# The gate/up stage of a hybrid decoder layer: chunk 3 in place of chunk 7 as the one split by an accumulating DMA

## Chip, cores and metric

The kernel runs on one core of one Trainium2 chip. The metric is the device time of one execution in microseconds, as the median of several runs. TensorE (PE) does the matrix products, DVE (VectorE), ACT (ScalarE) and POOL (GpSimd) work on the operands, SP (SyncE) issues most transfers.

## What is computed

One decoder layer for 256 tokens of width 2048, all in float32: an input projection, three kinds of token mixing, an output projection, and then the feed-forward part, which the change touches:

```python
h = rms_norm(x, ffn_norm)
return x + (jax.nn.silu(h @ w_gate) * (h @ w_up)) @ w_down
```

D_FF is 5632, so w_gate and w_up are 2048 x 5632 each and w_down is 5632 x 2048. A final RMS norm follows.

## The kernel before

**Three products for one.** TensorE multiplies in the format fp32r. To keep float32's accuracy each operand is split: hi = the value rounded to fp32r, lo = value - hi. A product is then three matmuls: x_hi with w_hi, x_hi with w_lo, x_lo with w_hi (`group`, L1665 to L1673). The weights come from memory as raw float32. ScalarE copies raw to hi (`prep_hi`, L739 and L743), DVE subtracts to make lo (`prep_lo`, L1239 and L1261).

**The gate/up stage.** It runs over FS = 11 iterations, i = 0 to 10, each for 512 columns of w_gate and the same of w_up. An iteration has FB = 8 chunks, p = 0 to 7. A chunk is 1 MB of weights (128 partitions x 4 blocks x 512 columns). Banks 0 to 3 of PSUM gather gate and up for the two halves of the tokens, bank[0] and bank[1] the gate, bank[2] and bank[3] the up part.

**Sums chunks.** Chunks 0, 2, 4, 5 (`SUMS`) are done with seven block products in place of eight, by Winograd's form of Strassen's scheme: 7 x 3 = 21 matmuls (`sums_chunk`). For this DVE first adds blocks of raw weights (L1251, L1254, L1256, into t_sum), ScalarE makes t_hi of them (L747), and DVE t_lo (L1266): the "tops". The three bare blocks get w_hi by L743 and w_lo by L1261. A sums chunk adds into banks 0 to 2 and 4 to 7. When the last of the four is done, banks 4 to 7 must be mixed: ScalarE copies bank 4 (L864), DVE makes the mix sums (`mix_sums`, L1354, L1356, L1359) and corrects banks 0 and 1, then 2 and 3 (`mix_banks`, L1369). TensorE waits for the first correction (`mixed`) before the first product of chunk 7, and for the second before its third.

**Plain chunks.** The others (1, 3, 6, 7) are 24 matmuls each (`plain_chunk`).

**The ring.** Raw weights have four slots, and so have w_hi and w_lo (w_lo lies over raw). `ring(n)` is the number of chunk n within the ring, `slot_user(n)` the chunk that had its slot before; SP issues a load (L397) when TensorE has used that chunk (`chunk_used`). SP does its loads strictly in the written order. AHEAD = 3 is how many chunks ScalarE and DVE prepare ahead of TensorE.

**The chunk set apart.** Chunk 7 (`BY_DMA`) of each iteration isn't in the ring. SP loads it into d_raw (L407), ScalarE makes d_hi (`apart_hi`, L844), then writes -d_hi into d_lo (`apart_negated`, L849; d_lo lies over d_raw), and GpSimd issues a DMA that reads the chunk from memory once more and adds it to d_lo (L479). What it leaves is lo, without any work of DVE. TensorE waits for `lo_added`. In the kernel before all this is done within the iteration: d_raw is loaded when the iteration before is used up, and ScalarE does its two steps beside chunks 3 to 5.

**End of an iteration.** When chunk 7 has filled a bank, ScalarE makes the gate (L870, Silu), DVE multiplies it with the up part (L1454). In the next iteration TensorE turns this tile after chunk 0 and within chunk 1 (`hidden_turn`, L1564), and ScalarE stores it (`keep_hidden`, L816).

**Down stage.** 44 chunks m of w_down go through the same ring (`down_hi`, `down_lo`). Chunk 0 is a sums chunk whose sums are made at the end of iteration 10. After the load of down chunk 3 SP waits for the end of the gate/up stage and brings back x (2 MB, x_keep, L423), which was put away to make room for d_raw, d_lo and d_hi.

## Time and profile before

| | us |
|---|---|
| median of 3 runs | 1106.45 |
| lowest, highest | 1102.81, 1107.13 |
| the profiled execution, its time | 1107.73 |
| the profiled execution, its span | 1105.2 |
| TensorE busy | 1083.0 (98%) |
| DVE busy | 909.5 (82%) |
| ScalarE busy | 652.5 (59%) |

The granted TensorE clock is 0.995 of full on the mean. The gate/up stage runs from about 387 to 866 us of the span, the down stage from there to the end. Busy shares tell little here, since TensorE is busy nearly always: the profile is read by its waits, by who releases them, and by what that engine did before. In a timeline row the bracket at the end holds the idle time before the instruction and its releaser; "PE" rows are matmuls, "SPq" rows the issue of a transfer, and "128x2048 fp32r<-128x2048 f32" is result and source.

### The profile page before, as it was taken

What the parts mean: (1) busy time and instruction counts of PE and PEld (TensorE: products, weight loads), DVE (VectorE), ACT (ScalarE), POOL (GpSimd) and SP (SyncE); (2) the same over time, 40 slices, a digit from 0 to 9 for tenths busy, and PEclk for the clock granted to TensorE, in tenths of its full rate; (3) what the DMA queues carried; (4) which work ended last, traced back from release to release, by engine and by line L of the source; (5) the groups of instructions that cost most, each with busy time, mean ns of one, the idle gap of its engine ahead of it and who ended that gap; (6) DMA issues with size and microseconds to landing.
All of it is one profiled execution on the core that took longest, in us unless ns stands there. A gap on an engine that the chain in (4) does not pass through costs nothing.

```text
span 1105.2 us, 12406 instructions
## 1 busy us (share of the span) xinstructions
PE 1083.0 (98%) x5094; PEld 898.8 (81%) x5094; DVE 909.5 (82%) x858; ACT 652.5 (59%) x639; POOL 57.4 (5%) x55
## 2 busy tenths in 40 slices
PE   9999999999999998999999999999999999999997
PEld 6888889987888877877887887887888788888886
DVE  6889666754666798898898898998998799998995
ACT  7666446656655565664664664655657455565553
POOL 0078000000000000000000000000000000000000
PEclk9999999999999999999999999999999999999999
DMA  8765644653445586766766757757667665555552
GB/s 330 278 232 201 201 120 137 199 174 118 143 162 191 191 304 196 244 193 232 239 196 222 243 198 245 224 194 243 205 228 237 233 210 205 190 195 206 208 192 113
DMA packets 50439, 228.55 MB, mean 207 GB/s; under 512 B 4304, under 2 KB 10192, under 8 KB 28752
## 3 DMA queue, kind: packets, MB, share of 16 engines
q1 hardware_dynamic: 47936, 213.84, 55.8%
q0 software_dynamic: 1584, 11.54, 5.6%
q10 hardware_dynamic: 864, 2.39, 0.6%
q8 instruction: 40, 0.66, 0.2%
q14 instruction: 15, 0.12, 0.0%
HBM read 223.56 MB, written 4.19 MB: 206 GB/s over the span
## 4 chain that ended last, share of the span: by engine, by line
PE 82%; DMA 6%; DVE 5%; issue 3%; ACT 3%; SPq 0%; DVEq 0%; ACTq 0%
PE ps L1672 61%; PE ps L1525 5%; PE ps L1527 5%; PE ps L1526 5%; DMA raw<-in_w_gu 5%; PE ps L1564 2%; ACT w_hi L739 1%; DMA d_raw<-in_w_gu 1%; DVE mix L1356 1%; DVE t_sum L1251 1%; DVE ps L1369 1%; PE ps L1612 1%; PE ps L1789 1%; PE ps L1790 1%; PE ps L1791 1%
## 5 line engine op out<-in xcount | busy, mean ns | idle before, releaser
L1672 PE MATMUL ps<-w_hi,xp_hi 128*128 128x512 f32 x396 | 156.1, 394 | 3.0 <-DVE t_lo L1266 3.0
L966 DVE TENSOR_TENSOR w_lo<-raw,w_hi 128x2048 fp32r<-128x2048 f32 (+2 forms) x42 | 87.3, 2078 | 86.6 <-ACT w_hi L490 86.6
L1672 PE MATMUL ps<-w_hi,xp_lo 128*128 128x512 f32 x396 | 154.3, 390 | 0.0
L1672 PE MATMUL ps<-w_lo,xp_hi 128*128 128x512 f32 x396 | 154.2, 389 | 0.0
L747 ACT ACTIVATE t_hi<-t_sum 128x2048 fp32r<-128x2048 f32 x44 | 84.4, 1917 | 90.9 <-DVE t_sum L1256 90.9
L830 ACT ACTIVATE w_hi<-raw 128x2048 fp32r<-128x2048 f32 (+1 forms) x44 | 79.2, 1800 | 77.6 <-DMA raw<-in_w_dn 77.6
L1672 PE MATMUL ps<-w_hi,xo_hi 128*128 128x512 f32 x292 | 113.8, 390 | 0.0
L1672 PE MATMUL ps<-w_hi,xo_lo 128*128 128x512 f32 x292 | 113.6, 389 | 0.0
L1672 PE MATMUL ps<-w_lo,xo_hi 128*128 128x512 f32 x292 | 113.6, 389 | 0.0
L1266 DVE TENSOR_TENSOR t_lo<-t_sum,t_hi 128x2048 fp32r<-128x2048 f32 x44 | 100.8, 2290 | 12.0 <-ACT t_hi L747 12.0
L490 ACT ACTIVATE w_hi<-raw 128x2048 fp32r<-128x2048 f32 (+2 forms) x42 | 73.0, 1739 | 49.5 <-DMA raw<-in_w_out 25.8
L1239 DVE TENSOR_TENSOR w_lo<-raw,w_hi 128x2048 fp32r<-128x2048 f32 x33 | 75.6, 2290 | 22.6 <-ACT w_hi L739 22.6
L1672 PEld LDWEIGHTS ps<-w_hi,xp_hi 128*128 128x128 f32 x396 | 74.5, 188 | 18.1 <-DVE t_lo L1266 3.4
L1672 PEld LDWEIGHTS ps<-w_hi,xp_lo 128*128 128x128 f32 x396 | 74.3, 188 | 15.7
L1672 PEld LDWEIGHTS ps<-w_lo,xp_hi 128*128 128x128 f32 x396 | 74.4, 188 | 14.9
L1384 DVE TENSOR_TENSOR w_lo<-raw,w_hi 128x2048 fp32r<-128x2048 f32 x32 | 73.2, 2288 | 14.4 <-ACT w_hi L830 14.3
L1261 DVE TENSOR_TENSOR w_lo<-raw,w_hi 128x1536 fp32r<-128x1536 f32 x44 | 77.3, 1756 | 2.1 <-ACT w_hi L743 1.0
L743 ACT ACTIVATE w_hi<-raw 128x1536 fp32r<-128x1536 f32 x44 | 65.4, 1487 | 22.8 <-DMA raw<-in_w_gu 22.8
L739 ACT ACTIVATE w_hi<-raw 128x2048 fp32r<-128x2048 f32 x33 | 63.0, 1909 | 26.0 <-DMA raw<-in_w_gu 26.0
L1672 PE MATMUL ps<-t_hi,xp_hi 128*128 128x512 f32 x176 | 69.1, 392 | 0.4 <-DVE xp_lo L1208 0.4
L1672 PE MATMUL ps<-t_hi,xp_lo 128*128 128x512 f32 x176 | 69.2, 393 | 0.0
L1672 PE MATMUL ps<-t_lo,xp_hi 128*128 128x512 f32 x176 | 69.2, 393 | 0.0
(294 smaller groups left out, 2471.0 us busy)
## 6 DMA issues: line engine op xcount, KB each, us to landing
raw<-in_w_gu SPq DMA_DIRECT2D x77, 1024.0 KB, 4.9
raw<-in_w_dn SPq DMA_DIRECT2D x44, 1024.0 KB, 4.9
raw<-in_w_i SPq DMA_DIRECT2D x21, 1024.0 KB, 4.9
raw<-in_w_out SPq DMA_DIRECT2D x16, 1024.0 KB, 5.2
raw<-in_w_in SPq DMA_DIRECT2D x12, 1024.0 KB, 5.1
d_raw<-in_w_gu SPq DMA_DIRECT2D x11, 1024.0 KB, 4.9
d_lo<-in_w_gu POOLq DMA_DIRECT2D x11, 1024.0 KB, 9.1
raw<-in_w_in SPq DMA_DIRECT2D x8, 576.0 KB, 3.8
```

Source lines behind the costliest of these rows:

```text
L490: nc.scalar.activation(w_hi[n % 4][:, 0:k, 0:c], raw[n % 4][:, 0:k, 0:c], ACT.Copy).then_inc(hi_ready, 1)
L739: nc.scalar.activation(w_hi[slot][:], raw[slot][:], ACT.Copy).then_inc(hi_ready, 1)
L743: nc.scalar.activation(w_hi[slot][:, 1:4, :], raw[slot][:, 1:4, :], ACT.Copy).then_inc(hi_ready, 1)
L747: nc.scalar.activation(t_hi[s % 2][:], t_sum[s % 2][:], ACT.Copy).then_inc(tops_hi, 1)
L830: nc.scalar.activation(w_hi[slot][:, blocks, :], raw[slot][:, blocks, :], ACT.Copy).then_inc(hi_ready, 1)
L966: nc.vector.tensor_tensor(w_lo[n % 4][:, 0:k, 0:c], raw[n % 4][:, 0:k, 0:c], w_hi[n % 4][:, 0:k, 0:c].bitcast(F32), ALU.subtract).then_inc ...
L1239: nc.vector.tensor_tensor(w_lo[slot][:], raw[slot][:], w_hi[slot][:].bitcast(F32), ALU.subtract).then_inc(lo_ready, 1)
L1261: nc.vector.tensor_tensor(w_lo[slot][:, 1:4, :], raw[slot][:, 1:4, :], w_hi[slot][:, 1:4, :].bitcast(F32), ALU.subtract)
L1266: nc.vector.tensor_tensor(t_lo[s][:], t_sum[s][:], t_hi[s][:].bitcast(F32), ALU.subtract).then_inc(lo_ready, 1)
L1384: nc.vector.tensor_tensor(w_lo[slot][:], raw[slot][:], w_hi[slot][:].bitcast(F32), ALU.subtract).then_inc(lo_ready, 1)
L1525: nc.tensor.matmul(out, hi, w_h, start=start, stop=False)
L1672: mm = nc.tensor.matmul(out, x, wt, start=start and j + m == 0, stop=stop and 3 * j + m == n - 1, skip_group_check=resumed)
```

## The change

Chunk 3 in place of chunk 7 is set apart, in iterations 1 to 10. In iteration 0 all eight chunks go through the ring, so that there are ten accumulating DMAs in place of eleven. The chunk of iteration i + 1 is prepared in iteration i: SP loads d_raw behind the load of chunk 7, when chunk 3 has been used; ScalarE does apart_hi before its copy of bank 4 and the negation behind it; GpSimd's DMA follows. The ring has chunks 0 to 2 and 4 to 7 in each iteration from 1 on. The loops of ScalarE and DVE over p are written out in another order: DVE does all low parts of an iteration, then the mix sums, then the next iteration's sums of chunk 0, the first correction, the low part of its bare blocks, the second correction, the tops, the gates, and only then chunk 1. Before, the next iteration's sums stood ahead of the mix sums, its bare low part ahead of both corrections, and chunk 1 ahead of the gates.

Core of the diff (the first hunks: constants, ring, SP, GpSimd; then ScalarE's ffn, DVE's prep_lo and ffn, TensorE's):

```diff
-BY_DMA = 7
+BY_DMA = 3
...
-    return n - sum(FF0 + BY_DMA + FB * i < n for i in range(FS))
+    return n - sum(FF0 + BY_DMA + FB * i < n for i in range(1, FS))
...
-    return next(m for m in range(n) if ring(m) == r and not (FF0 <= m < DN0 and (m - FF0) % FB == BY_DMA))
+    return next(m for m in range(n) if ring(m) == r and not (FF0 + FB <= m < DN0 and (m - FF0) % FB == BY_DMA))
...
-                if i == 0:
+                if i == 1:
                     sp.wait_ge(x_kept, 16)
                     sp.wait_ge(unit_filled, len(ORDER))
                     sp.wait_ge(nx2.squared, 8)
                 else:
-                    sp.wait_ge(chunk_used, FF0 + FB * i)
+                    sp.wait_ge(chunk_used, FF0 + FB * (i - 1) + BY_DMA + 1)
                 sp.dma_start(d_raw[:].rearrange("p a b -> p (a b)").unsqueeze(1),
                              w_gu[:, FB * i + BY_DMA:FB * i + BY_DMA + 1, :]).then_inc(d_in, 16)
 
             for i in range(FS):
                 for p in range(FB):
-                    if p != BY_DMA:
+                    if i == 0 or p != BY_DMA:
                         load_ring(FF0 + FB * i + p, w_gu[:, FB * i + p:FB * i + p + 1, :])
                     if i == 0 and p == 3:
                         sp.wait_ge(acc_free, ACC_O + 8)
                         sp.dma_start(t["x_keep"], xin[:].rearrange("p a b -> p (a b)")).then_inc(x_kept, 16)
-                    if p == (5 if i == 0 else 3):
-                        load_apart(i)
+                    if p == FB - 1 and i + 1 < FS:
+                        load_apart(i + 1)
...
-            for i in range(FS):
-                pool.wait_ge(negated, i + 1)
+            for i in range(1, FS):
+                pool.wait_ge(negated, i)
...
-                act.wait_ge(d_in, 16 * (i + 1))
+                act.wait_ge(d_in, 16 * i)
...
-                act.wait_ge(d_hi_made, i + 1)
+                act.wait_ge(d_hi_made, i)
...
-                        nc.scalar.activation(mix[:, 0, :], bank[4], ACT.Copy).then_inc(mix_first, 1)
...
-                    q = p + AHEAD
-                    if q == BY_DMA:
-                        if last:
-                            down_hi(0, "b")
-                        else:
-                            prep_hi(i, FB, "b")
...
-                        prep_hi(i, q, "b")
-                        if p == (2 if first else 1):
-                            apart_negated(i)
-                        prep_hi(i, q, "t")
...
-                    if p == (1 if first else 0):
-                        apart_hi(i)
+                if first:
+                    for j, u in enumerate(UNITS[FF0]):
+                        act.wait_ge(unit_filled, INDEX[u] + 1)
+                        split_pair_hi(u, late_bank[j])
+                    prep_hi(i, 2, "t")
+                    prep_hi(i, 3)
+                    root(nx2, 1, D)
+                else:
+                    keep_hidden(i, (0,))
+                    prep_hi(i, 2, "t")
+                    keep_hidden(i, (1,))
+                prep_hi(i, 4)
+                if first:
+                    prep_hi(i, 5)
+                    prep_hi(i, 6)
+                else:
+                    prep_hi(i, 5, "b")
+                    prep_hi(i, 6)
+                    prep_hi(i, 5, "t")
+                prep_hi(i, 7)
+                if not first and not last:
+                    apart_hi(i + 1)
+                act.wait_ge(mix_done, i * 2 + 1)
+                if not first:
+                    act.wait_ge(mixed, i * 2)
+                nc.scalar.activation(mix[:, 0, :], bank[4], ACT.Copy).then_inc(mix_first, 1)
+                if not first and not last:
+                    apart_negated(i + 1)
+                if last:
+                    down_hi(0)
+                else:
+                    prep_hi(i, FB)
+                if first:
+                    apart_hi(i + 1)
+                    apart_negated(i + 1)
+                    act.wait_ge(nx2.ready, 1)
+                for b in range(TOK):
+                    act.wait_ge(ffn_done, i * 3 + (b + 1))
+                    nc.scalar.activation(gate[:, b, :], bank[b], ACT.Silu,
+                                         scale=nx2.r[:, b:b + 1]).then_inc(gate_set, 1)
+                if last:
+                    down_hi(1)
+                    down_hi(2)
+                else:
+                    prep_hi(i, FB + 1)
+                    prep_hi(i, FB + 2, "b")
 
...
+                    if q == SUMS[2]:
+                        dve.wait_ge(chunk_used, i * FB + (FF0 + SUMS[0] + 1))
...
-                    if p == SUMS[-1]:
-                        ahead = (lambda parts: down_lo(0, parts)) if last else (lambda parts: prep_lo(i, FB, parts))
-                        ahead("s")
-                        mix_sums(i)
-                        ahead("w")
-                        mix_banks(i, 0, None)
-                        mix_banks(i, 1, i * FB + (FF0 + 7))
-                        ahead("l")
-                    if p == FB - 1:
-                        for b in range(TOK):
-                            dve.wait_ge(gate_set, i * 2 + (b + 1))
-                            if b == 0:
-                                dve.wait_ge(ffn_done, i * 3 + 3)
-                            else:
-                                dve.wait_ge(chunk_used, i * FB + (FF0 + FB))
-                            nc.vector.scalar_tensor_tensor(out=gate[:, b, :], in0=bank[2 + b],
-                                                           scalar=nx2.r[:, b:b + 1], in1=gate[:, b, :],
-                                                           op0=ALU.mult, op1=ALU.mult).then_inc(hid_made, 1)
-                    if p + AHEAD > FB and last:
-                        down_lo(p + AHEAD - FB)
-                    elif p + AHEAD not in (BY_DMA, FB):
-                        prep_lo(i, p + AHEAD)
...
+                else:
+                    prep_lo(i, 2)
+                for p in range(4, FB):
+                    prep_lo(i, p)
+                mix_sums(i)
+                ahead = (lambda parts: down_lo(0, parts)) if last else (lambda parts: prep_lo(i, FB, parts))
+                ahead("s")
+                mix_banks(i, 0, None)
+                ahead("w")
+                mix_banks(i, 1, i * FB + (FF0 + 7))
+                ahead("l")
+                for b in range(TOK):
+                    dve.wait_ge(gate_set, i * 2 + (b + 1))
+                    if b == 0:
+                        dve.wait_ge(ffn_done, i * 3 + 3)
+                    else:
+                        dve.wait_ge(chunk_used, i * FB + (FF0 + FB))
+                    nc.vector.scalar_tensor_tensor(out=gate[:, b, :], in0=bank[2 + b],
+                                                   scalar=nx2.r[:, b:b + 1], in1=gate[:, b, :],
+                                                   op0=ALU.mult, op1=ALU.mult).then_inc(hid_made, 1)
+                if last:
+                    down_lo(1)
+                    down_lo(2)
+                else:
+                    prep_lo(i, FB + 1)
...
-                w_h, w_l = (d_hi, d_lo) if p == BY_DMA else (m[ring(FF0 + FB * i + p) % 4] for m in (w_hi, w_lo))
+                w_h, w_l = (d_hi, d_lo) if p == BY_DMA and not first else (m[ring(FF0 + FB * i + p) % 4] for m in (w_hi, w_lo))
-                    if p == BY_DMA:
-                        pe_.wait_ge(lo_added, 16 * (i + 1))
+                    if p == BY_DMA and not first:
+                        pe_.wait_ge(lo_added, 16 * i)
```

DVE, before, from the plain low part of chunk 6 of one iteration to its gates; L1239 is a plain low part, L1251 to L1256 are sums, L1354 to L1359 mix sums, L1369 corrections, L1454 gates:

```order
L1239 TENSOR_TENSOR w_lo_54<-raw_50,w_hi_58 128x2048
L1251 TENSOR_TENSOR t_sum_61<-raw_51 128x1024
L1254 TENSOR_TENSOR t_sum_61<-t_sum_61,raw_51 128x512
L1256 TENSOR_TENSOR t_sum_61<-t_sum_61,raw_51 128x512
L1354 TENSOR_TENSOR mix<-mix,ps 128x512
L1356 TENSOR_TENSOR mix<-ps,mix 128x1024
L1359 TENSOR_TENSOR mix<-ps,mix 128x512
L1261 TENSOR_TENSOR w_lo_55<-raw_51,w_hi_59 128x1536
L1369 TENSOR_TENSOR ps<-ps,mix 128x1024 x2
L1266 TENSOR_TENSOR t_lo_63<-t_sum_61,t_hi_65 128x2048
L1239 TENSOR_TENSOR w_lo_56<-raw_52,w_hi_60 128x2048
L1454 SCALAR_TENSOR_TENSOR gate<-ps,stats,gate 128x512 x2
```

DVE, after, from the plain low part of chunk 6 on (L1356 to L1361 are now the mix sums, L1253 to L1258 sums, L1263 the bare low part, L1371 a correction):

```order
L1239 TENSOR_TENSOR w_lo_54<-raw_50,w_hi_58 128x2048
L1239 TENSOR_TENSOR w_lo_55<-raw_51,w_hi_59 128x2048
L1356 TENSOR_TENSOR mix<-mix,ps 128x512
L1358 TENSOR_TENSOR mix<-ps,mix 128x1024
L1361 TENSOR_TENSOR mix<-ps,mix 128x512
L1253 TENSOR_TENSOR t_sum_61<-raw_52 128x1024
L1256 TENSOR_TENSOR t_sum_61<-t_sum_61,raw_52 128x512
L1258 TENSOR_TENSOR t_sum_61<-t_sum_61,raw_52 128x512
L1371 TENSOR_TENSOR ps<-ps,mix 128x1024
L1263 TENSOR_TENSOR w_lo_56<-raw_52,w_hi_60 128x1536
L1371 TENSOR_TENSOR ps<-ps,mix 128x1024
L1268 TENSOR_TENSOR t_lo_63<-t_sum_61,t_hi_65 128x2048
```

Behind the plain low parts the mix sums now come first, and the first correction stands directly behind the next sums; chunk 7's low part is a second L1239 ahead of them.

ScalarE, before, from its second keep_hidden of an iteration on; L844 and L849 are the two steps for the chunk set apart, L864 the copy of bank 4:

```order
L816 ACTIVATE hid<-ps 128x512
L844 ACTIVATE d_hi<-d_raw 128x2048
L743 ACTIVATE w_hi_58<-raw_50 128x1536
L849 ACTIVATE d_lo<-d_hi 128x2048
L747 ACTIVATE t_hi_65<-t_sum_61 128x2048
L743 ACTIVATE w_hi_59<-raw_51 128x1536
L747 ACTIVATE t_hi_66<-t_sum_62 128x2048
L739 ACTIVATE w_hi_60<-raw_52 128x2048
L743 ACTIVATE w_hi_57<-raw_49 128x1536
L864 ACTIVATE mix<-ps 128x512
L747 ACTIVATE t_hi_65<-t_sum_61 128x2048
L739 ACTIVATE w_hi_58<-raw_50 128x2048
```

ScalarE, after, from the tops of chunk 4 on (L877 is the copy of bank 4, L890 the gates):

```order
L747 ACTIVATE t_hi_65<-t_sum_61 128x2048
L743 ACTIVATE w_hi_59<-raw_51 128x1536
L739 ACTIVATE w_hi_60<-raw_52 128x2048
L747 ACTIVATE t_hi_66<-t_sum_62 128x2048
L739 ACTIVATE w_hi_57<-raw_49 128x2048
L844 ACTIVATE d_hi<-d_raw 128x2048
L877 ACTIVATE mix<-ps 128x512
L849 ACTIVATE d_lo<-d_hi 128x2048
L743 ACTIVATE w_hi_58<-raw_50 128x1536
L747 ACTIVATE t_hi_65<-t_sum_61 128x2048
L890 ACTIVATE gate<-ps,stats 128x512 x2
L739 ACTIVATE w_hi_59<-raw_51 128x2048
```

The two steps for the chunk set apart moved from beside chunks 3 to 5 to both sides of the copy of bank 4, behind the high part of chunk 7 and ahead of that of the next chunk 0.

## Rows read from the trace of the kernel before

**Rows 1.** Table of waits, TensorE: total us, times, longest.

```profile
PE ps L1672 <- DVE ps L1369: 8.3, 6, 1.9
```

**Rows 2.** Timeline, TensorE: start us, length us, ..., [idle before <- releaser]; iterations 0, 5, 6, 10.

```profile
417.92 0.50 PE L1672 MATMUL ps<-w_hi,xp_hi 128*128 128x512 f32 x1 [3.01 <-DVE t_lo L1266]
...
419.80 0.63 PE L1672 MATMUL ps<-t_hi,xp_hi 128*128 128x512 f32 x1
420.23 0.63 PE L1672 MATMUL ps<-t_lo,xp_hi 128*128 128x512 f32 x1
...
642.59 0.39 PE L1672 MATMUL ps<-w_lo,xp_hi 128*128 128x512 f32 x1
642.82 0.39 PE L1672 MATMUL ps<-w_hi,xp_lo 128*128 128x512 f32 x1
643.23 0.47 PE L1672 MATMUL ps<-d_hi,xp_hi 128*128 128x512 f32 x1
...
686.95 0.47 PE L1672 MATMUL ps<-d_hi,xp_hi 128*128 128x512 f32 x1 [1.71 <-DVE ps L1369]
...
858.83 0.47 PE L1672 MATMUL ps<-d_hi,xp_hi 128*128 128x512 f32 x1 [1.89 <-DVE ps L1369]
```

**Rows 3.** Timeline, DVE, before chunk 7 of iteration 6.

```profile
676.53 2.29 DVE L1239 TENSOR_TENSOR w_lo<-raw,w_hi 128x2048 fp32r<-128x2048 f32 x1 [3.05 <-ACT w_hi L739]
678.74 1.22 DVE L1251 TENSOR_TENSOR t_sum<-raw 128x1024 f32<-128x1024 f32 x1
...
681.33 0.68 DVE L1354 TENSOR_TENSOR mix<-mix,ps 128x512 f32<-128x512 f32 x1
...
683.91 1.75 DVE L1261 TENSOR_TENSOR w_lo<-raw,w_hi 128x1536 fp32r<-128x1536 f32 x1
685.58 2.36 DVE L1369 TENSOR_TENSOR ps<-ps,mix 128x1024 f32<-128x1024 f32 x2
```

**Rows 4.** Timeline, GpSimd, SyncE and ScalarE: loads around the accumulating DMA.

```profile
662.87 0.86 POOL L479 DMA_DIRECT2D d_lo<-in_w_gu  x1 [41.54 <-ACT d_lo L849]
...
664.87 0.33 SPq L397 DMA_DIRECT2D raw<-in_w_gu  x1
...
670.31 0.33 SPq L397 DMA_DIRECT2D raw<-in_w_gu  x1
...
674.58 1.92 ACT L739 ACTIVATE w_hi<-raw 128x2048 fp32r<-128x2048 f32 x1 [3.43 <-DMA raw<-in_w_gu]
677.70 1.49 ACT L743 ACTIVATE w_hi<-raw 128x1536 fp32r<-128x1536 f32 x1 [1.20 <-DMA raw<-in_w_gu]
```

**Rows 5.** The page, DMA issues: KB each, median us to landing.

```profile
d_raw<-in_w_gu SPq DMA_DIRECT2D x11, 1024.0 KB, 4.9
```

**Rows 6.** Timeline, DVE: low part of the tops.

```profile
664.31 2.29 DVE L1266 TENSOR_TENSOR t_lo<-t_sum,t_hi 128x2048 fp32r<-128x2048 f32 x1 [0.59 <-ACT t_hi L747]
```

**Rows 7.** Timeline, ScalarE and DVE, iteration 0.

```profile
408.64 1.93 ACT L844 ACTIVATE d_hi<-d_raw 128x2048 fp32r<-128x2048 f32 x1 [2.52 <-DMA d_raw<-in_w_gu]
...
431.47 1.28 ACT L870 ACT_TABLE_LOAD   x1 [4.46 <-PE ps L1672]
...
408.36 1.22 DVE L1251 TENSOR_TENSOR t_sum<-raw 128x1024 f32<-128x1024 f32 x1
...
415.58 2.29 DVE L1266 TENSOR_TENSOR t_lo<-t_sum,t_hi 128x2048 fp32r<-128x2048 f32 x1 [1.78 <-ACT t_hi L747]
```

**Rows 8.** Down chunk 4: stretch (last column GB/s), then ScalarE, DVE, TensorE timelines.

```profile
866.00:878.00 12.00, 12.00 (x58) 9.97 (x57) 5.96 (x6) 5.46 (x7) 0.00 (x0) 1.00 0.87 311
...
878.13 1.49 ACT L830 ACTIVATE w_hi<-raw 128x1536 fp32r<-128x1536 f32 x1 [1.99 <-DMA raw<-in_w_dn]
...
878.47 1.22 DVE L1400 TENSOR_TENSOR t_sum<-raw 128x1024 f32<-128x1024 f32 x1
...
886.52 0.68 DVE L1429 TENSOR_TENSOR xo_lo<-sf,xo_hi 128x512 fp32r<-128x512 f32 x1
...
888.02 0.39 PE L1672 MATMUL ps<-w_hi,xo_hi 128*128 128x512 f32 x1
```

54 lines of the change are left out of this document (10 added, 44 removed).

## Prediction

> **What bounds the kernel now.** I read the table of waits first, since TensorE is busy for nearly the whole span: only what it still waits for can be gained. DVE's bank correction (L1369) holds it 8.3 us in six waits, five in iterations 1 to 9 of the gate/up stage and one in iteration 10 [rows 1]. Then TensorE's own timeline [rows 2]. A matmul lasts 0.39 us, but the next one starts after 0.23 (642.59, 642.82), so an idle time of x costs x + 0.16. The first matmul of chunk 7 starts 0.41 after the last of chunk 6 in iteration 5 (643.23), 0.18 lost; in iteration 6 (686.95) the idle time is 1.71, about 1.9 lost. Iterations 1 to 10 go on like that: six waits (8.3 + 6 x 0.16 = 9.2) and four small ones of 0.18 to 0.29 (1.0 together), in all 10.2, of which the last (858.83, 1.89 idle) has 2.05. Iteration 0 has another, 3.01 idle at 417.92, for the tops of chunk 5. Behind this one and behind 858.83 the matmuls go at 0.43 us each for a while (419.80, 420.23), which is the lower level of the clock: nine matmuls each time, 9 x 0.2 = 1.8 us. Behind the idle time of 1.71 none do.
>
> Why is the correction late? DVE's rows in iteration 6 [rows 3]: it stands 3.05 us before the low part of chunk 6, then does the next iteration's sums (678.74), the mix sums (681.33), the next low part (683.91), and only then the correction (685.58). So the 3.05, and 2.6 + 1.7 of work for the next iteration, stand ahead of what TensorE wants. The 3.05 is a transfer's [rows 4]: chunk 6 was issued at 664.87, two microseconds behind the accumulating DMA (662.87), and landed at 674.58, 9.7 later; the median is 4.9 [rows 5].
>
> **The yardstick.** A sums chunk is 21 matmuls x 0.227 = 4.76 us, a plain one 24 x 0.227 = 5.44; with 1.0 for the two turns an iteration is 4 x 4.76 + 4 x 5.44 + 1.0 = 41.8. Chunks 0 to 7 begin at T = 0, 5.2, 11.2, 16.0, 21.4, 26.2, 30.9, 36.4. DVE's steps: a plain low part 2.2 (676.53 to 678.74), sums 2.6 to 2.7, mix sums 2.6, bare low part 1.7, a correction 1.15 (two in 2.36) [rows 3]; before the tops a wait for ScalarE of 0.2 to 0.6, and their low part 2.2 [rows 6]. A sums chunk is thus about 7.0, a gate product 0.7. Per iteration 3 x 2.2 + 4 x 7.0 + 2.6 + 2.3 + 1.4 = 40.9 of 41.8: it fits, narrowly.
>
> **Iterations 1 to 9 with the change.** No work is added in them. The second gate product needs all of the chunk 7 before, so DVE starts at T = 0.1. It ends the gate at 0.8, chunk 1 at 3.0, chunk 2 at 10.2 (7.2, because keep_hidden stands before its tops on ScalarE); TensorE wants chunk 2 at 11.2. Chunk 4 ends at 17.2 (wanted 21.4), 5 at 24.2 (26.2), 6 at 26.4, 7 at 28.6. The mix sums want ScalarE's copy, which now stands behind apart_hi: d_raw is issued at 21.7, lands 4.9 later at 26.6 [rows 5], apart_hi takes until 28.5, the copy until 29.1. Mix sums to 31.7, next sums to 34.3, first correction to 35.5, wanted at 36.4; low part and second correction to 38.3, wanted at 39.1; tops of the next chunk 0 to 40.5, in time for the gates. The three narrow margins are 1.0, 0.9 and 0.8. For what is left of waits I take 0.1 per iteration, between nothing and the 0.18 of 643.23. Saved: 10.2 - 2.05 = 8.2, less 0.9, **7.3**. Bounds: 8.2, and nothing if the loads of the next paragraph are late.
>
> The moved DMA could eat this. It goes out behind the negation, at 31.4, beside the load of the next chunk 1 (31.2) and ahead of those of chunk 2 (36.6) and 4 (42.0). ScalarE wants chunk 1 at 40.7, and the margins bear it up to 41.5. The nearest rows are 4.9 and the 9.7 of old chunk 6 [rows 4, 5]: it lands between 36.1 and 40.9. I take it near 40.9, since the two transfers run together, and that is still in time. Chunk 2 is wanted at 44.8, 8.2 after its issue; the second load behind the DMA took 7.4 in the old order (670.31 to 677.70) [rows 4].
>
> A rule speaks against this. The Trainium skill (DMA: Bandwidth & Descriptors, Queues, rings and completion order) says that each DMA engine takes turns, packet by packet, between the queues that have work. A load issued together with the accumulating DMA would then share with it to the end, and be as late as the DMA itself. That is rival A, priced below from rows.
>
> **Iteration 0.** Before, ScalarE waited 2.52 us for d_raw (408.64) and did apart_hi and the negation ahead of the tops of chunk 5, which DVE began at 415.58, after 1.78 of waiting; TensorE wanted them at 417.92 - 3.17 = 414.75 [rows 2, 7]. Both steps and their transfers leave this place, and DVE goes on from the sums of chunk 5 (408.36) directly: 2.7 + 1.7 + 0.3 + 2.2, done at 415.3, wait 0.6. Then chunks 6 and 7 (2 x 2.2), mix sums, next sums and correction: 415.3 + 4.4 + 2.6 + 2.6 + 1.15 = 426.0, wanted at 415.35 + 4.76 + 5.44 = 425.5, wait 0.4, and 0.1 at the second one. Here the low part of chunk 7 is the added work (its other half was the DMA's), and it is on the path. ScalarE has the next sums at 424.7; tops, apart_hi and negation (1.8 each), the table load and the gates (1.3 each) [rows 7] end at 432.7, the high part of chunk 1 at 434.5, DVE's low part at 436.8 (wait 0.1), chunk 2 at 443.6, wanted at 442.8 (0.8). Together 2.0 to 2.1 instead of 3.2 + 1.8: saved **2.9**; bounds 5.0 (no wait) and 0.
>
> **Iteration 10.** The next sums are those of the down stage: three operations more (1.0), and 0.6 for the activations' low part before the second correction. Corrections at 36.5 (0.2 late) and 39.9 (0.7 late). It was 2.05 and 1.8 of slow clock: saved 3.85 - 0.9 = **2.95**, or 1.1 if the slow clock remains.
>
> **Down stage: a cost.** With chunk 7 in the ring, SP issues the down stage's chunk 3 when chunk 7 is used, no longer when chunk 6 is, and the return of x_keep, 2 MB, stands right behind it, then down chunk 4. Before, the return went out alone at the end of chunk 7 and down chunk 4 landed at 878.13 [rows 8]. From 866 to 878 the engines moved 311 GB/s on the mean, so one MB in front is up to 1.05/0.311 = 3.4 us; I take 3.0. Down chunk 4 was ready at 887.2 (886.52 + 0.68) for a first matmul at 888.02, 0.8 of margin, and its sums began 0.35 behind the landing (878.47). So 3.0 - 0.35 - 0.8 = **1.8** lost. Bounds 0 (other order in the queue) and 2.3.
>
> **Sum.** 7.3 + 2.9 + 2.95 - 1.8 = 11.35. The profiled execution took 1107.73 us (span 1105.2), so 1096.4 for it; it stands 1.28 over the median of the three runs, 1106.45, which becomes **1095.1**. All waits gone and no new one: 8.2 + 5.0 + 3.85 = 17.0, at 1089.4. A change within 0.5% (5.5 us: 1100.9 to 1112.0) is about what a measurement of this kernel can't tell from none.
>
> The slow stretches are 3.6 of the waits I let go, on the reading that long waits bring them: 1.71 of idle time brought none, 1.89 did [rows 2]. The Trainium skill (TensorE: Matmul & The Clock Gate, What's actually happening) says that the gate looks in windows that run freely, so one execution can fall into it where another doesn't; by that the 3.6 could stay, at 1098.7, and the two rows can't exclude it.
>
> **Rivals.**
> A, chunk 1 is late by the accumulating DMA. The nearest row for "as late as the DMA" is 662.87 to 674.58, 11.7 us with one load inside; a start together is shorter by part of it. Taken to land at 42.1 (10.9 after issue), it is 0.6 over the 41.5 that the margins bear, in each of nine iterations in place of 0.1: 9 x 0.5 = 4.5, at 1099.6. For it: 9.7 is already near 10.3. Against: old chunk 6 started two microseconds worse placed.
> B, DVE stays the bound. 40.9 of 41.8 leaves 0.9; if ScalarE's tops come 0.25 later in each sums chunk it is gone, and the period stays near the 42.9 that it has on the mean. Only iterations 0 and 10 gain and the down stage loses: 2.9 + 2.95 - 1.8 = 4.05, at 1102.4, no change.
> C, slower. The accumulating DMA holds the load of chunk 2 as well. Chunk 2 bears 8.2 + 1.0 = 9.2 us from issue to landing; beyond, all goes into TensorE's wait, nine times. 11.35/9 = 1.3 more is parity, a load of 10.5. At 11.7, the longest stretch from the DMA's issue to a landing behind it [rows 4], it is 9 x 2.5 = 22.5, at 1117.6. Against: the 7.4 of such a load.
> D, the change doesn't do what it says, since ScalarE's copy for the mix sums now hangs on d_raw. The correction bears 0.9; if d_raw lands two microseconds late, as old chunk 6 did by more, 9 x 1.1 = 10 are lost, at 1105. Against: at 21.7 the loads ahead have landed.
>
> **How the numbers follow.** Forecast (1090 to 1098) 0.52; A 0.22; B 0.12; D 0.06; C 0.08. The range leaves out C, D, a little of B and of the low end: 1090.5 to 1103. Faster by over 0.5%: the forecast, most of A and a little of B, 0.70; slower 0.08; no change 0.22.
>
> **What would show it.** Right: no idle time at chunk 7 in iterations 1 to 9, and a period of 41.8 to 41.9; a wait of 1 to 2 us at down chunk 4, its load landing some 15 us behind the end of chunk 7. Wrong: waits at chunk 1 or 2, with DVE waiting for ScalarE and ScalarE for a transfer (A, C); ScalarE idle before apart_hi and TensorE at chunk 7 (D); matmuls at 0.43 us behind no long wait (the free-running gate). What decides above all is how long the loads beside the accumulating DMA take.

## The result, and the profile after

| | before | after |
|---|---|---|
| median, us (5 runs each) | 1106.45 | 1095.2 |
| lowest, highest | 1102.81, 1107.72 | 1095.0, 1097.15 |
| time over time of before, 95% interval | | 0.9905 (0.9887 to 0.9923) |
| the profiled execution: time, span | 1107.73, 1105.2 | 1095.72, 1093.4 |
| granted clock, mean | 0.995 | 0.999 |

The forecast was 1095.1, within 1090.5 to 1103. The kernel is 1.0% faster, within the class "faster by over 0.5%". The same kernel run a second time, beside other kernels, gave 1095.93 (1095.3 to 1097.19).

The page of after: engines (busy, share, instructions), and the DMA issues with their size and time to landing.

```profile
PE 1078.3 (99%) x5094; PEld 896.6 (82%) x5094; DVE 911.8 (83%) x859; ACT 652.9 (60%) x638; POOL 55.7 (5%) x54
...
raw<-in_w_gu SPq DMA_DIRECT2D x78, 1024.0 KB, 5.0
...
d_raw<-in_w_gu SPq DMA_DIRECT2D x10, 1024.0 KB, 4.8
d_lo<-in_w_gu POOLq DMA_DIRECT2D x10, 1024.0 KB, 11.7
```

The table of TensorE's waits in after (sum, times, longest), to lay beside [rows 1]:

```profile
PE ps L1676 <- DVE xo_lo L1431: 2.1, 1, 2.1
...
PE ps L1676 <- DVE ps L1371: 0.7, 3, 0.3
PE ps L1676 <- DVE t_lo L1268: 0.7, 2, 0.5
...
PE ps L1676 <- DVE w_lo L1239: 0.2, 1, 0.2
PE ps L1676 <- ACT hid L816: 0.2, 1, 0.2
```

The 8.3 us of the bank correction are 0.7 in three waits, the 3.0 of the tops are 0.7 in two, and a new line of 2.1 stands on top, the one forecast at the down stage's chunk 4. Where these lie, in TensorE's own timeline of after; from 400 to 905 us they are all:

```profile
415.51 0.50 PE L1676 MATMUL ps<-w_hi,xp_hi 128*128 128x512 f32 x1 [0.47 <-DVE t_lo L1268]
...
426.32 0.47 PE L1676 MATMUL ps<-w_hi,xp_hi 128*128 128x512 f32 x1 [0.27 <-DVE ps L1371]
...
437.50 0.50 PE L1676 MATMUL ps<-w_hi,xp_hi 128*128 128x512 f32 x1 [0.24 <-DVE w_lo L1239]
...
442.52 0.50 PE L1676 MATMUL ps<-w_hi,xp_hi 128*128 128x512 f32 x1 [0.18 <-ACT hid L816]
...
444.37 0.51 PE L1676 MATMUL ps<-w_hi,xp_hi 128*128 128x512 f32 x1 [0.19 <-DVE t_lo L1268]
...
845.65 0.47 PE L1676 MATMUL ps<-w_hi,xp_hi 128*128 128x512 f32 x1 [0.17 <-DVE ps L1371]
...
848.96 0.50 PE L1676 MATMUL ps<-w_hi,xp_hi 128*128 128x512 f32 x1 [0.30 <-DVE ps L1371]
...
876.15 0.47 PE L1676 MATMUL ps<-w_hi,xo_hi 128*128 128x512 f32 x1 [2.07 <-DVE xo_lo L1431]
```

Between 444.37 and 845.65 there is none: iterations 2 to 9 run without a gap, one every 41.74 us. By the start-to-start times these eight waits cost 5.2 us, where before lost 16.6 in that stretch with its slow matmuls. Taken whole, from the first product of chunk 0 in iteration 0 (394.93 before, 395.06 after) to that of down chunk 4 (888.02, 876.15), before needs 493.1 us and after 481.1. So the 12.0 between the two profiled executions (1107.73 - 1095.72) all lie here, 11.4 of them in the listed waits and the slow matmuls. From 400 us on no matmul of after goes at 0.43 us.

Now DVE in iteration 6, the counterpart of [rows 3]; the iteration's first matmul is at 642.06:

```profile
665.91 4.49 DVE L1239 TENSOR_TENSOR w_lo<-raw,w_hi 128x2048 fp32r<-128x2048 f32 x2
671.15 0.69 DVE L1356 TENSOR_TENSOR mix<-mix,ps 128x512 f32<-128x512 f32 x1 [0.75 <-PE ps L1676]
...
673.74 1.22 DVE L1253 TENSOR_TENSOR t_sum<-raw 128x1024 f32<-128x1024 f32 x1
...
676.33 1.23 DVE L1371 TENSOR_TENSOR ps<-ps,mix 128x1024 f32<-128x1024 f32 x1
677.46 1.75 DVE L1263 TENSOR_TENSOR w_lo<-raw,w_hi 128x1536 fp32r<-128x1536 f32 x1
679.13 1.23 DVE L1371 TENSOR_TENSOR ps<-ps,mix 128x1024 f32<-128x1024 f32 x1
680.26 2.28 DVE L1268 TENSOR_TENSOR t_lo<-t_sum,t_hi 128x2048 fp32r<-128x2048 f32 x1
682.71 0.75 DVE L1462 SCALAR_TENSOR_TENSOR gate<-ps,stats,gate 128x512 f32<-128x512 f32 x1 [0.17 <-PE ps L1676]
684.07 0.75 DVE L1462 SCALAR_TENSOR_TENSOR gate<-ps,stats,gate 128x512 f32<-128x512 f32 x1 [0.61 <-PE ps L1676]
684.74 2.28 DVE L1239 TENSOR_TENSOR w_lo<-raw,w_hi 128x2048 fp32r<-128x2048 f32 x1
```

The 3.05 us in front of the low part of chunk 6 are gone. What DVE waits for is now TensorE: 0.75 before the mix sums, 0.17 and 0.61 before the gates. An engine that waits for the one that bounds the kernel is off the path, so this small idle time should be the margin that the new order has; two runs below test it.

ScalarE at the end of iteration 5 and the beginning of 6, where the moved transfer would show (GpSimd issued it at 631.25):

```profile
640.13 1.91 ACT L739 ACTIVATE w_hi<-raw 128x2048 fp32r<-128x2048 f32 x1
645.30 1.49 ACT L743 ACTIVATE w_hi<-raw 128x1536 fp32r<-128x1536 f32 x1 [3.27 <-DMA raw<-in_w_gu]
```

The first is the next chunk 1, which follows the gates without a wait. Its load was issued at 631.37, 0.12 us behind the accumulating DMA. Its row in SyncE's timeline, and the landing of the two from the DMA issues between 631.3 and 631.5:

```profile
631.37 0.33 SPq L397 DMA_DIRECT2D raw<-in_w_gu  x1
...
d_lo<-in_w_gu POOLq DMA_DIRECT2D x1, 1024.0 KB, 12.5
raw<-in_w_gu SPq DMA_DIRECT2D x1, 1024.0 KB, 5.8
```

The load is there at 637.2, 3 us before ScalarE comes to it, while the DMA beside it takes 12.5. The second is chunk 2, issued at 636.81: ScalarE stands 3.27 for its transfer, which lands 8.5 after its issue, and DVE's sums begin at the same 645.30, right behind the low part of chunk 1 (643.00 + 2.28). It lands just as DVE asks for it.

### The profile page after: what moved, and what is told of

It reads as the page before. It is cut to its first block, busy times and chain, and to the rows that moved or that the text cites. A ratio compares the mean times of both kernels' runs of the same rounds, so it can differ in the third digit from the quotient of the medians.

```text
span 1093.4 us, 12415 instructions
## 1 busy us (share of the span) xinstructions
PE 1078.3 (99%) x5094; PEld 896.6 (82%) x5094; DVE 911.8 (83%) x859; ACT 652.9 (60%) x638; POOL 55.7 (5%) x54
## 4 chain that ended last, share of the span: by engine, by line
PE 88%; DVE 6%; ACT 2%; DMA 2%; issue 1%; SPq 0%; DVEq 0%; ACTq 0%
PE ps L1676 67%; PE ps L1529 5%; PE ps L1531 5%; PE ps L1530 5%; PE ps L1568 2%; DMA raw<-in_w_dn 1%; DVE w_lo L1239 1%; DVE t_lo L1268 1%; ACT t_hi L747 1%; PE ps L1616 1%; DVE t_sum L1253 1%; PE ps L1793 1%; PE ps L1795 1%; PE ps L1794 1%; PE ps L1615 0%
## 5 line engine op out<-in xcount | busy, mean ns | idle before, releaser
L1676 PE MATMUL ps<-w_hi,xp_hi 128*128 128x512 f32 x404 | 159.8, 395 | 1.8 <-DVE ps L1371 0.7
L1676 PE MATMUL ps<-w_hi,xp_lo 128*128 128x512 f32 x404 | 157.5, 390 | 0.0
L1676 PE MATMUL ps<-w_lo,xp_hi 128*128 128x512 f32 x404 | 157.4, 390 | 0.0
L1239 DVE TENSOR_TENSOR w_lo<-raw,w_hi 128x2048 fp32r<-128x2048 f32 x34 | 76.7, 2284 | 1.8 <-ACT w_hi L739 1.8
L1263 DVE TENSOR_TENSOR w_lo<-raw,w_hi 128x1536 fp32r<-128x1536 f32 x44 | 77.3, 1756 | 1.1
L1676 PEld LDWEIGHTS ps<-w_hi,xo_hi 128*128 128x128 f32 x292 | 54.8, 188 | 13.8 <-DVE t_lo L1428 2.5
## 6 DMA issues: line engine op xcount, KB each, us to landing
d_lo<-in_w_gu POOLq DMA_DIRECT2D x10, 1024.0 KB, 11.7
```

The costliest lines, as they stand in the source:

```text
L1239: nc.vector.tensor_tensor(w_lo[slot][:], raw[slot][:], w_hi[slot][:].bitcast(F32), ALU.subtract).then_inc(lo_ready, 1)
L1263: nc.vector.tensor_tensor(w_lo[slot][:, 1:4, :], raw[slot][:, 1:4, :], w_hi[slot][:, 1:4, :].bitcast(F32), ALU.subtract)
L1676: mm = nc.tensor.matmul(out, x, wt, start=start and j + m == 0, stop=stop and 3 * j + m == n - 1, skip_group_check=resumed)
```

## The experiments

The question was which part of the change brings the gain of iterations 1 to 9: DVE's order, in which the correction no longer stands behind work for the next iteration, or the place of the accumulating DMA, which had run beside chunk 6's load. The prediction's sum takes the change as one schedule and doesn't tell them apart. The diffs are against the kernel named; the kernel before was run beside each group again (medians 1104.84 to 1105.9), and each ratio is to its own group's.

**DVE's order alone**, on before:

```diff
-                        ahead("s")
                         mix_sums(i)
-                        ahead("w")
+                        ahead("s")
                         mix_banks(i, 0, None)
+                        ahead("w")
                         mix_banks(i, 1, i * FB + (FF0 + 7))
```

> The kernel before with one thing of the change alone: DVE does the mix sums ahead of the next iteration's sums, and the first bank correction ahead of the next bare low part (chunk 7 stays the one set apart, within its iteration). Theory 1 (what stands ahead of the correction on DVE is half of the trouble): the correction comes 1.67 us earlier, the length of the bare low part. The six waits at chunk 7 (lost 0.96, 1.13, 1.38, 1.87, 1.83, 2.05) shrink to 0 to 0.4 each and the slow stretch behind the last one goes; the waits and slow stretch of iteration 0 (3.2 + 1.8) stay. 7 + 2 + 1.8 = about 10 us saved: 1096 to 1098, nearly the whole gain of the change. Theory 2 (the move of the transfer is what gains, DVE's order is secondary, since DVE's backlog only moves to the next wait): new waits at chunk 0 to 2 or at the second correction take most of it back, time 1102 to 1106.

Measured: 1116.91 us (1116.21 to 1118.34), 1.01 of before (1.0078 to 1.0121). A miss by 20 us, in sign too. Its waits of TensorE, DVE in iteration 6, and ScalarE there:

```profile
PE ps L1564 <- ACT hid L816: 10.4, 10, 1.1
PE ps L1672 <- DVE ps L1369: 7.1, 10, 1.9
```

```profile
682.03 2.29 DVE L1239 TENSOR_TENSOR w_lo<-raw,w_hi 128x2048 fp32r<-128x2048 f32 x1 [3.24 <-ACT w_hi L739]
684.75 0.69 DVE L1354 TENSOR_TENSOR mix<-mix,ps 128x512 f32<-128x512 f32 x1 [0.43 <-ACT mix L864]
```

```profile
658.11 1.92 ACT L747 ACTIVATE t_hi<-t_sum 128x2048 fp32r<-128x2048 f32 x1 [5.87 <-DVE t_sum L1256]
659.93 0.58 ACT L816 ACTIVATE hid<-ps 128x512 f32<-128x512 f32 x1
...
680.08 1.92 ACT L739 ACTIVATE w_hi<-raw 128x2048 fp32r<-128x2048 f32 x1 [3.62 <-DMA raw<-in_w_gu]
682.75 1.49 ACT L743 ACTIVATE w_hi<-raw 128x1536 fp32r<-128x1536 f32 x1 [0.75 <-DMA raw<-in_w_gu]
684.14 0.58 ACT L864 ACTIVATE mix<-ps 128x512 f32<-128x512 f32 x1
```

The transfer still holds DVE 3.24 at chunk 6, so the work that was moved from before the correction is done behind it, and the next iteration starts late. There ScalarE keeps the hidden layer (L816) only behind tops for which it waits 5.87 on DVE, and the turn of TensorE waits for that, ten times 1.0. And ScalarE's copy of bank 4 (L864) stands behind the next chunk's high part. Of the two theories the second had the mechanism, DVE's backlog moving to the next wait, but neither had the size. The order is worth nothing while the transfer is late: it hands the debt on.

**The move alone**, after with before's order of DVE:

```diff
-                mix_sums(i)
                 ahead = (lambda parts: down_lo(0, parts)) if last else (lambda parts: prep_lo(i, FB, parts))
                 ahead("s")
-                mix_banks(i, 0, None)
+                mix_sums(i)
                 ahead("w")
+                mix_banks(i, 0, None)
                 mix_banks(i, 1, i * FB + (FF0 + 7))
```

> The changed kernel with the old order on DVE at the end of an iteration: next sums, mix sums, next bare low part, then both corrections. Theory 1: the next chunk 0 is now loaded when chunk 4 is used (T = 26.4) and lands at 31.4, 2.8 us after DVE is through with chunk 7; with its sums ahead of the mix sums the correction ends at 31.4 + 2.7 + 2.6 + 1.7 + 1.15 = 39.5 against 36.4 wanted, so TensorE waits some 3 us at chunk 7 of every iteration: 10 x 3 = 30 us, time about 1125, and up to 15 more if each such wait brings a slow stretch of 1.8 us. Theory 2 (the transfer's place is what counts): the period stays within 0.5 us of 41.75 and the time within 5 us of the changed kernel's, 1095 to 1100.

Measured: 1148.08 us (1138.11 to 1158.6), 1.035 of before (1.0296 to 1.0398). The granted clock was 0.991 in the profiled execution, the one of 1138.11, and 0.983 to 0.967 in the three others; the expectation's 1125 to 1140 holds for the first alone. The wait, its first case with what follows, and DVE's sums for the next chunk 0 before the fourth:

```profile
PE ps L1676 <- DVE ps L1371: 34.3, 11, 4.4
```

```profile
429.09 0.47 PE L1676 MATMUL ps<-w_hi,xp_hi 128*128 128x512 f32 x1 [2.83 <-DVE ps L1371]
...
430.15 0.63 PE L1676 MATMUL ps<-w_lo,xp_hi 128*128 128x512 f32 x1
430.57 0.63 PE L1676 MATMUL ps<-w_hi,xp_lo 128*128 128x512 f32 x1
...
475.57 0.47 PE L1676 MATMUL ps<-w_hi,xp_hi 128*128 128x512 f32 x1 [2.87 <-DVE ps L1371]
...
557.48 1.23 DVE L1253 TENSOR_TENSOR t_sum<-raw 128x1024 f32<-128x1024 f32 x1 [3.05 <-DMA raw<-in_w_gu]
```

Ten waits of 2.8 to 3.2 and one of 4.4, as expected: with chunk 7 in the ring the load of the next chunk 0 goes out later (here at 552.46) and lands 3.05 us after DVE is through with chunk 7, and the old order has the sums of this chunk ahead of the mix sums, so the correction stands behind that transfer. So the new order is needed by the move, and pays nothing without it. The waits sum to 34.3; with slow matmuls the time is more than that. Matmuls at 0.43 us follow five of the eleven waits (2.83, 3.07, 3.16, 3.02, 4.40) and not the six others (2.87 to 3.11), as the first and the second here.

**The DMA taken away**, in before and in after: it moves 64 of the 2048 columns, and the low part of its chunk is left out for the rest.

```diff
-                pool.dma_start(d_lo[:].rearrange("p a b -> p (a b)"), w_gu[:, FB * i + BY_DMA, :],
+                pool.dma_start(d_lo[:].rearrange("p a b -> p (a b)")[:, 0:64], w_gu[:, FB * i + BY_DMA, 0:64],
```

> The kernel before with the accumulating DMA cut to 64 of 2048 columns (the low part of chunk 7 is left out for the rest: that part of the computation is missing, all instructions and waits stay). Theory: it is this DMA that holds the load of chunk 6 for 9.7 us in place of 4.9; without it chunk 6 lands at 5, DVE's idle 3.05 us ahead of its low part goes, and with it all waits at chunk 7: 10.2 + 1.8 saved less 0.2 to 0.5 in iteration 10, time 1094 to 1096. The wait of iteration 0 stays, since ScalarE waits there for d_raw, not for the sum. Rival: the load of chunk 6 is slow for another reason (memory, its place in the queue) or DVE's own work is the bound: then time stays at 1104 to 1107 and the 3.05 us remain.

> The changed kernel with the accumulating DMA cut in the same way (low part of chunk 3 left out). Theory: in the new place it costs nothing: ScalarE's wait of 3.27 us before chunk 2 shrinks, but TensorE waits for nothing there already, so the time stays at 1095 within 1 us. Rival: part of the period still hangs on it (waits hidden in the pace), then 1 us or more is gained.

Measured: before without it 1094.75 (1093.98 to 1098.39), 0.9902 of before; after without it 1097.56 (1095.41 to 1098.05), 0.9917 (0.9897 to 0.9936), beside 0.9905 with it. That is no faster than after; its median lies 2.4 over after's, with a granted clock of 0.997 in the three slower of its four runs, while the profiled one (1095.41) has the gaps of after to 0.03 us and the same period of 41.74. In before's place the DMA costs 11 us, in after's nothing that these runs show. Before without it, the rows that answer to [rows 3]:

```profile
667.47 2.29 DVE L1239 TENSOR_TENSOR w_lo<-raw,w_hi 128x2048 fp32r<-128x2048 f32 x1
...
679.31 1.23 DVE L1369 TENSOR_TENSOR ps<-ps,mix 128x1024 f32<-128x1024 f32 x1 [1.49 <-PE ps L1672]
```

No 3.05 in front of chunk 6, whose load takes 4.8 to 5.7 us in iterations 1 to 10 in place of 8.0 to 9.7, and in the old order the second correction waits for TensorE, though the mix sums stand behind the next sums as ever. In iterations 1 to 9 TensorE waits for no correction any more. So the whole cause of those waits is the transfer beside chunk 6's load. (Of the 3.01 at chunk 5 of iteration 0, 1.8 stay.)

**Order and ScalarE, without the move**: the first experiment, with its ScalarE faults mended (copy of bank 4 ahead of the next chunk 0's high part, the kept hidden layer ahead of the tops).

```diff
+                        prep_hi(i, 2, "t")
...
-                            prep_hi(i, FB, "b")
...
-                            prep_hi(i, FB, "t")
+                            prep_hi(i, FB)
...
+                    elif q == FB + 2:
+                        prep_hi(i, q, "b")
```

> As e1 (the kernel before with the mix sums and the first correction earlier on DVE), and ScalarE's queue put in the changed kernel's order at the two places where e1 waited: the copy of bank 4 ahead of the next chunk 0's high part, and the storing of the turned tile (keep_hidden) ahead of chunk 2's tops. Chunk 7 is still the one set apart, within its iteration. Theory (in e1 TensorE waited 10 times 1.25 us at the second turn, for keep_hidden that stood behind tops for which DVE was late): these 10 waits go, 12.5 us, but the load of chunk 6 still lands 10 to 11 us after its issue, DVE stays late, and 0.5 to 1 us at chunk 7 remain in each iteration: about 1104, no better than before. Rival (the two places on ScalarE were all that e1 lacked, and the move of the chunk isn't needed): 1095 to 1098.

Measured: 1106.26 (1101.87 to 1108.46, 10 runs), 0.9999 of before (0.9984 to 1.0013). The rival's 1095 to 1098 is excluded. The load of chunk 6 still takes 9.2 to 10.7 us in iterations 1 to 10, DVE waits 2.90 for it in iteration 6, and TensorE 4.4 in six corrections:

```profile
675.16 2.29 DVE L1239 TENSOR_TENSOR w_lo<-raw,w_hi 128x2048 fp32r<-128x2048 f32 x1 [2.90 <-ACT w_hi L739]
```

```profile
PE ps L1672 <- DVE ps L1369: 4.4, 6, 1.6
```

**How much room is there beside the moved DMA?** It is made twice in a row:

```diff
+                pool.wait_ge(lo_added, 32 * i - 16)
+                pool.dma_start(d_lo[:].rearrange("p a b -> p (a b)"), w_gu[:, FB * i + BY_DMA, :],
+                               accum_op=ALU.add).then_inc(lo_added, 16)
```

> After, with the accumulating DMA of each iteration made twice, the second behind the end of the first (the low part of bank 4's weight is then added twice, so the result is another one). It stretches the time in which a second transfer runs beside the loads of the next iteration's chunks 1, 2 and 4, from 11.7 us to over 20. If the DMA's fit depends on what it shares the engines with (rival A of the prediction, with chunk 2's load as its victim: DVE takes it the moment it lands, at 645.3): that load lands about 2 us later, chunk 2 waits 1 to 2 us in each of nine iterations, and the run takes 1105 to 1114. If the loads have room left at this place: 1096 to 1098, and no wait at chunk 2 above 0.3.

Measured: 1098.76 (1098.28 to 1099.63), 0.9939 of before (0.9917 to 0.9962), 3.6 us over after and 0.8 over the expected range. The two land 12.5 us behind their issues on the median, one after the other. All that it costs is one wait, in iteration 1, for the DMA itself:

```profile
451.86 0.50 PE L1679 MATMUL ps<-d_hi,xp_hi 128*128 128x512 f32 x1 [2.01 <-DMA d_lo<-in_w_gu]
```

and the slow matmuls behind it (1.6 us): iteration 1 takes 47.16 us there, 43.20 in after. Chunk 2 of iteration 6 is read 14.40 us behind the first DMA's issue (635.47 to 649.87) instead of 14.05 (631.25 to 645.30), and TensorE waits nowhere in iterations 2 to 9. But this doesn't test rivals A and C. The second DMA goes out 11.2 to 13.2 us behind the first; chunk 1's load had landed by then, and chunk 2's met it for a microsecond or two at most. What runs beside the second are the loads of chunks 4, 5 and 6: they take up to 10.7 us in place of 5 to 7, and TensorE waits for none of them. The room that the run shows is theirs.

**How much room does DVE have?** One operation more in an iteration, then two longer ones. The first:

```diff
+                    if not first:
+                        nc.vector.tensor_tensor(xf[:, 4:8, :], xf[:, 0:4, :], xf[:, 0:4, :], ALU.max)
                     prep_lo(i, FB + 1)
```

The second, in which the first operation is made over all eight blocks, and another stands ahead of chunk 5:

```diff
                 for p in range(4, FB):
+                    if p == 5 and 1 < i < FS - 1:
+                        nc.vector.tensor_tensor(xf[:, 0:8, :], xf[:, 0:8, :], xf[:, 0:8, :], ALU.max)
```

> After with one more DVE operation of 0.7 us (128x512 maximum, on a tile that is free) per iteration, ahead of chunk 1's low part, in iterations 1 to 9. From 605 to 647 DVE idles 0.83 ahead of the mix sums and 0.17 + 0.61 ahead of the gates, 1.61 in a period. If that idle time is real room: the operation is swallowed before the mix sums, 1095 to 1096.5. If the gate/up stage is still bound by DVE (rival B) the period grows by 0.7: 9 x 0.7 = 6.3, 1102.

> The same with two operations of 1.23 us (128x1024 maximum) per iteration, one ahead of chunk 1's low part (iterations 1 to 9) and one ahead of chunk 5's (2 to 9), 2.46 in place of 0.7. That is over the 1.61 of idle time by 0.85: about 8 x 0.85 = 7 more, 1101 to 1105, with the waits of TensorE at the corrections or at the next chunk 0. If there is more room than the idle time shows: under 1099. If DVE bounds already: 17 x 1.23 = 21, at 1116.

Measured: 1095.46 (1094.89 to 1096.58) and 1102.29 (1101.12 to 1103.3). The first is swallowed, the period still 41.74. The second has a period of 42.51, 0.77 longer, for 0.85 expected; in eight iterations that is 6.2 of the 6.8 by which it stands over the operation of 0.7 us. A period (columns: length, busy time and count of PE, PEld, DVE, ACT, POOL, then granted clock, DMA share, GB/s); first after, then with two operations:

```profile
605.44:647.18 41.74, 41.74 (x192) 34.57 (x190) 39.08 (x30) 25.49 (x18) 0.86 (x1) 1.00 0.73 228
```

```profile
529.40:571.90 42.50, 42.32 (x189) 34.35 (x189) 41.15 (x33) 25.50 (x18) 0.88 (x1) 1.00 0.71 222
```

And a row of TensorE's timeline with two:

```profile
554.80 0.47 PE L1680 MATMUL ps<-w_hi,xp_hi 128*128 128x512 f32 x1 [0.18 <-DVE ps L1371]
```

It is a wait for a correction, 0.18 to 0.22 idle and 0.33 to 0.38 lost in each iteration: the waits come back at the place where they were. The rest of the 0.77 is in losses of about 0.1 each. So the 1.61 us of idle time that DVE's rows show are its margin, right to about 0.1 (2.46 - 0.77 = 1.69).

**The return of x_keep**: after, with it in four pieces behind the down stage's chunks 6, 8, 10 and 12, and final_norm's 1 MB issued beside chunk 12 in place of chunk 0 (not in the lines below).

```diff
-                if m == 3:
-                    sp.wait_ge(chunk_used, DN0)
-                    sp.dma_start(xin[:].rearrange("p a b -> p (a b)"), t["x_keep"]).then_inc(x_back, 16)
+                if m in (6, 8, 10, 12):
+                    c = (m - 6) * 512
+                    sp.dma_start(xin[:].rearrange("p a b -> p (a b)")[:, c:c + 1024],
+                                 t["x_keep"][:, c:c + 1024]).then_inc(x_back, 16)
```

> The changed kernel with x brought back later and in four pieces of 512 KB (behind the loads of down chunks 6, 8, 10, 12) and final_norm's 1 MB issued beside down chunk 12 in place of 0. Theory: the load of down chunk 4 then takes some 5 us in place of 10, the wait of 2.07 us at down chunk 4 goes and none comes in its place: 2.2 us less than the changed kernel, 1093. Rival (the pieces hold other loads and the wait only moves): 1095.

Measured: 1094.27 (1094.18 to 1094.69), 0.9899 of before (0.9886 to 0.9913), span 1091.9 against 1093.4. That is 0.9 under after, or 1.7 under after as run beside it (1095.93); the 1093 was missed by 1.3. In the profiles the down stage's matmuls take 232.3 us from first to last in place of 234.3. The load of down chunk 4 takes 5.1 us, the wait at this chunk is gone, and no new one is listed behind it. Two transfers were moved, so the run doesn't tell apart the share of the return and that of final_norm's load.

**The ends of the stage too**: that kernel, and in iteration 0 ScalarE's apart_hi and negation around the copy and DVE's first correction ahead of the next sums; in iteration 10 the down stage's activation sums and low part behind the corrections. Then the ScalarE part alone.

```diff
+                if first:
+                    apart_hi(i + 1)
...
-                    apart_hi(i + 1)
-                    apart_negated(i + 1)
...
+                if first:
+                    mix_banks(i, 0, None)
+                    ahead("s")
+                    mix_banks(i, 1, i * FB + (FF0 + 7))
+                    ahead("w")
```

> As e6, and the order at both ends of the gate/up stage: in iteration 0 ScalarE does its two steps for the chunk set apart behind the copy of bank 4 (in its idle time before the next chunk 0's load lands), and DVE both corrections ahead of what they stood behind; in iteration 10 DVE does the activations' three sums behind the corrections. Theory: waits of 0.43, 0.23, 0.34, 0.36 (iterations 0 and 1) and 0.33, 0.46 (iteration 10) go, 2.1 us with the 2.2 of e6: 1091. Rival: in iteration 0 the accumulating DMA now runs beside the loads of chunks 1 and 2 and brings the waits back, 1092 to 1093.

> After with the return of x_keep in four pieces behind down chunks 6, 8, 10 and 12, and in iteration 0 ScalarE makes bank 4's high part and negation right around the copy, ahead of the gates and their table load (DVE as it was). The first alone gave 1094.27. Of the two waits of 0.62 and 0.43 at the end of iteration 0, the 0.43 goes if ScalarE's order is its cause, the 0.62 stays (that one is DVE's own backlog), and no wait appears at the next chunk 0: 1093.5 to 1094. If DVE's order was what brought the new 0.90 in the experiment on both, this run has none of it; if ScalarE's was, the 0.75 idle behind t_lo comes again and the time is 1094.3 or more.

Measured: 1092.47 (1092.39 to 1093.33) and, with ScalarE's part alone, 1092.61 (1091.74 to 1093.38), 0.988 of before (0.9857 to 0.9904). The first was expected at 1091 and lost part of its gain to two new waits:

```profile
431.93 0.50 PE L1687 MATMUL ps<-w_hi,xp_hi 128*128 128x512 f32 x1 [0.75 <-DVE t_lo L1269]
...
850.50 0.47 PE L1687 MATMUL ps<-w_hi,xo_hi 128*128 128x512 f32 x1 [0.87 <-DVE t_lo L1431]
```

The second has neither, so DVE's order brought them, and not the accumulating DMA as its rival had it: what was put behind the corrections was wanted right after. The second's own expectation, 1093.5 to 1094, was missed by 0.9 to the good: the 0.43 at chunk 7 of iteration 0 stays (0.46), while the three small waits of iteration 1 (437.50, 442.52, 444.37) go, which it hadn't counted on; this iteration takes 41.73 in place of 43.20 us. They came from ScalarE, whose tops, apart_hi, negation, table load and gates stood in a row ahead of chunk 1, as the prediction has it for the first of them. This is the fastest of the kernels run, 1.2% under before; the two are not told apart.

## Why the prediction was right

The forecast of 1095.1 stands beside 1095.2. That it is met to 0.1 is luck. To about 1 us it was worked out, but for what is said below of the moved DMA. The terms, by the starts of the first turn of an iteration (before: 440.07 in iteration 1, 825.24 in iteration 10, 870.76 in the down stage; after: 436.67, 813.78, 856.66) and of the two products named in the section on the result:

| saved, us | forecast | measured |
|---|---|---|
| iterations 1 to 9 | 7.3 | 9.5 |
| iteration 0, with what it leaves in iteration 1 | 2.9 | 2.1 |
| iteration 10 | 2.95 | 2.6 |
| down stage | -1.8 | -2.2 |
| sum | 11.35 | 12.0 |

Three terms were too hopeful and one too cautious, and the medians happen to differ by 11.25 where the profiled executions differ by 12.0.

**Iterations 1 to 9.** The waits went, and without the 0.9 that I had kept for small ones: iterations 2 to 9 have none. The nine periods take 385.2 us before. Nine of 41.74 are 9.5 less, more than the 8.2 that was the bound: x + 0.16 is the cost of a wait up to its end, and behind each the next matmul comes after 0.30 in place of 0.23, some 0.7 in nine. The period was worked out as 41.8 and is 41.74. DVE's schedule holds to a tenth. Counted from 642.06, the mix sums end at 31.7, the first correction at 35.4, the second at 38.2 and the tops at 40.5 (each the start of the row that follows, less its idle time); the prediction has 31.7, 35.5, 38.3 and 40.5. ScalarE's copy, feared in rival D, was done in time: DVE's mix sums waited for TensorE. What the sum of 40.9 in 41.8 called narrow was 1.6 to 1.7 us by the tests with added work: rival B was further off than 0.9.

**The moved DMA.** Here the number came out in spite of the reasoning. Taken: chunk 1's load lands near 40.9, since it runs together with the DMA; chunk 2's takes 7.4 to 8.2. Measured in iteration 5: chunk 1's goes out at 31.05 and lands at 36.8, 4 us earlier; chunk 2's takes 8.5 (7.8 to 8.9 in the nine iterations). The DMA lands 11.7 behind its issue, against 9.1 in its old place, and chunk 2's load takes longer than the plain 5.0, so transfers from two queues do hold each other up. But the load issued together with the DMA is done 6.7 us before it. By the Trainium skill's rule that rival A rests on (DMA: Bandwidth & Descriptors, Queues, rings and completion order: turns between the queues, packet by packet) it would be as late as the DMA; here the measurement differs.

What decides is the order of issue of the two, to within a microsecond. Over the traces of all runs with a DMA of full size, the 81 loads of 1 MB issued between 0.3 us ahead of it and 0.34 behind it took 5.6 to 6.8 us (in the run with two DMAs by the first); the 39 issued 0.9 to 2.4 behind it took 8.0 to 10.8. After has both: in iterations 1 to 9 chunk 1's load goes out 0.0 to 0.3 behind the DMA and takes 5.8 to 6.5, and behind the DMA of iteration 0 (431.06) a load issued 1.0 later takes 10.4. With 10.4, chunk 1's load would land at 41.5, exactly what the margins bear. So rival A was less than a microsecond of issue order away. The prediction has the two at 31.4 and 31.2 and makes nothing of it; that the rival stayed away was luck. Rival C wanted 10.5 us for chunk 2's load; the longest took 8.9.

**Iteration 0.** 2.0 to 2.1 left over by the sum; 0.62 + 0.43 + 0.48 + 0.34 + 0.36 = 2.2 measured in five waits (437.50 starts 0.83 behind the turn, 0.35 in iteration 5). The parts differ: the second correction wasn't late, chunk 1 lost 0.5 for a forecast of 0.1, chunk 2 lost 0.36 for 0.8, and the 0.34 for keep_hidden (442.52) weren't in the sum. **Iteration 10**: 0.2 + 0.7 forecast, 0.33 + 0.46. The slow clock cost 1.6 in each of the two places, for 1.8 taken: nine starts in 3.65 us in place of 2.04.

**The down stage** was the term that was sized too small: 1.8 taken, 2.23 lost (idle 2.07 at 876.15), with 2.3 as the bound. The transfers in question, SP's return and ScalarE's read of down chunk 4:

```profile
852.40 0.43 SPq L423 DMA_DIRECT2D xin<-x_keep  x1
```

```profile
867.26 1.49 ACT L830 ACTIVATE w_hi<-raw 128x1536 fp32r<-128x1536 f32 x1 [5.21 <-DMA raw<-in_w_dn]
```

The load lands 14.9 behind the return's issue, for "some 15". It lands 10.6 behind the stage's first turn, where before it was 7.4 (870.76 to 878.11): 3.2 later for 3.0 taken. And of the 0.8 of margin only 0.68 was there, since the first matmul starts 0.14 behind the end of xo_lo in after too (876.01 to 876.15). Together 3.2 - 0.35 - 0.68 = 2.2. The run with the return put off moved final_norm's load as well, which is issued at 859.13 and is in flight at the same time; it shows that the wait is of these two transfers, and not how much of it is the return's.

**The slow stretches.** 3.6 us of them (3.2 by the trace) were let go, and they went. That long waits bring them holds in part only. In the kernel with the move alone, waits of nearly the same length brought them or didn't (2.83 did, 2.87 and 3.11 didn't), 2.01 did at 451.86 in the run with the doubled DMA where the 2.07 at 876.15 in after didn't, and at chunk 5 of iteration 0 the 3.01 of before did and the 2.96 of DVE's order alone (418.07) didn't. The Trainium skill (TensorE: Matmul & The Clock Gate, What's actually happening) has the gate look in windows that run freely; by that rule waits of one length can fall either way, and these rows agree. It was right to let the 3.6 go because the waits of the gate/up stage themselves fell under 0.5: in none of the traces was an idle time under 1.89 followed by slow matmuls in the gate/up and down stages.

**Both parts were needed.** I had argued the sum as one schedule and would have expected 1096 to 1098 of the order alone. It gave 1116.9. The cause of the late correction is the DMA beside chunk 6's load; it can be taken away at its source (1094.75) or moved to where DVE doesn't wait (1095.2). The move needs the order, since the next chunk 0 then lands 3.05 us too late to stand ahead of the mix sums; the order alone only defers. In before the DMA goes out 2.0 to 2.4 us ahead of chunk 6's load in iterations 1 to 10. The rows on the order of issue suggest a cheaper cure, to hold the DMA there until this load has been issued; no run tries it.

## What to carry to other kernels

Ask of a late step which transfer holds the engine ahead of it, what runs beside that transfer and which of the two was issued first, before reordering the engine's work: reordering passes the debt to the next iteration. The room for work on an engine that isn't the bound is the idle time in a period that waits for the bounding engine, and it can be tested by putting a known operation in. When a ring gets another member, look at what stands behind it in the same queue: here the return of 2 MB came to stand right behind one load and ahead of the next, and 2.2 us were lost at the other end of the stage.

## What the runs showed of the hardware

The accumulating DMA of 1 MB takes 9.1 us to landing on the median of before, where the next loads go out some 2.2 and 7.6 us behind it, and 11.7 in after, where they go out 0.1, 5.6 and 11.1 behind; two in a row take 12.5 each. A plain load of 1 MB takes 4.8 to 5.0.

What a load beside it pays depends on when it is issued. Up to 0.34 us behind the DMA it takes 5.8 to 6.8, 0.9 to 2.4 us behind it 8.0 to 10.8 (chunk 6 in before: 9.7, and 3.05 of waiting on DVE), 5.2 to 5.9 us behind it 7.5 to 9.2. Two loads of one size, issued 1 us apart, thus differ by some 4 us. Two rows for it, 631.37 above with 5.8, and from the run with order and ScalarE the load issued at 662.78, 1.14 behind its DMA:

```profile
raw<-in_w_gu SPq DMA_DIRECT2D x1, 1024.0 KB, 10.4
```

Why the first microsecond decides stays open: the traces show when a transfer is issued and when it lands, and not what the engines do between. Nor does any run place a load between 0.34 and 0.88 us.
